# Moving the parameter and state rows ahead of the second weight unit, halving the first unit, and scaling one tile of x on ScalarE, in a hybrid decoder step

## The reference

```python
def mixer(h, conf_buf, ssm_buf, ssm_h, w_in, ...):
    proj = einsum('bld,de->ble', h, w_in)              # 1024 -> 2*1024 + 1024 + 1536 + 16 columns
    u = u_a * sigmoid(u_b)                             # conformer gate
    v, conf_buf_new = causal_dwconv(conf_buf, u, conf_dw_w, conf_dw_b)      # width 31
    v = silu(layernorm(v, conf_ln_g, conf_ln_b))
    xbc_c, ssm_buf_new = causal_dwconv(ssm_buf, xbc, ssm_conv_w, ssm_conv_b) # width 4
    y, h_new = ssd_scan(...)                           # chunked state-space scan
    out = einsum('ble,ed->bld', concat([v, y_ssm]), w_out)
    ...
x = x + mixer(rmsnorm(x, ln_mix))
x = x + hier_moe(rmsnorm(x, ln_ffn))                   # 32 experts of 3 x 1024 x 512, two per token
y = rmsnorm(x, ln_final)
```

## Time and profile before

| what | value |
|---|---|
| median of 3 runs | 794.14 us (793.25 to 794.57) |
| span of the profiled execution, first to last instruction | 789.4 us |
| TensorE busy in it | 757.8 us (96%), granted clock 0.987 in the mean |
| VectorE, ScalarE, GpSimd busy | 270.5, 154.4, 140.3 us |
| DMA | 249.58 MB, 316 GB/s in the mean |

### The profile page before, as it was taken

How to read it: one execution, slowest core, us unless ns; L and a number is a source line. 1 busy time by engine, 2 the same in 40 slices (tenths; PEclk the granted TensorE clock), 3 DMA queues, 4 the chain that set the end, 5 groups by cost and what they waited for, 6 DMA issues and landing times.

```text
span 789.4 us, 8694 instructions
## 1 busy us (share of the span) xinstructions
PE 757.8 (96%) x3470; PEld 360.5 (46%) x3470; DVE 270.5 (34%) x629; ACT 154.4 (20%) x308; POOL 140.3 (18%) x168
## 2 busy tenths in 40 slices
PE   6999999999999999799999999999999999989896
PEld 4667677767843335434333333333333333333332
DVE  2399499985656423511101101110110011011003
ACT  3211121245712003202011112101111110110122
POOL 2279998612002000100000000000000000000000
PEclk9999999999999999799999999999999999999998
DMA  9990610042659786999999999999999999999982
GB/s 312 304 364 10 230 40 1 9 107 108 188 213 275 252 306 237 368 374 414 429 426 427 425 429 425 425 430 426 427 427 426 425 426 427 427 429 425 429 356 69
DMA packets 51400, 249.58 MB, mean 316 GB/s; under 512 B 6982, under 2 KB 24422, under 8 KB 38671
## 3 DMA queue, kind: packets, MB, share of 16 engines
q1 hardware_dynamic: 45460, 243.40, 77.2%
q10 hardware_dynamic: 3371, 2.81, 1.2%
q0 software_dynamic: 2528, 2.79, 1.1%
HBM read 246.87 MB, written 8.61 MB: 324 GB/s over the span
## 4 chain that ended last, share of the span: by engine, by line
PE 91%; DMA 3%; DVE 2%; SPq 2%; issue 2%; ACT 1%; POOLq 0%; DVEq 0%
PE bank L1213 28%; PE bank L810 18%; PE bank L1236 14%; PE bank L1076 9%; PE bank L1261 9%; DMA xcx<-in_state_conf_conv 2%; PE bank L1196 2%; SPq L491 1%; PE bank L1225 1%; PE bank L1065 1%; PE bank L1034 1%; PE bank L905 1%; PE bank L1214 1%; PE bank L1122 1%; PE bank L1047 0%
## 5 line engine op out<-in xcount | busy, mean ns | idle before, releaser
L810 PE MATMUL bank<-region_a,ring 128*128 128x320 f32 x576 | 157.2, 433 | 1.0 <-DMA ring<-in_w_in 1.0
L1654 DVE TENSOR_TENSOR region_a<-region_a,bank 64x512 f32<-64x512 f32 (+1 forms) x33 | 22.5, 680 | 377.6 <-ACT region_a L1581 377.6
L1214 PE MATMUL bank<-ring,zz 128*64 128x512 f32 x320 | 145.4, 610 | 0.0
L1213 PE MATMUL bank<-ring,zz 128*64 128x512 f32 x288 | 127.3, 595 | 2.7 <-issue 2.7
L810 PEld LDWEIGHTS bank<-region_a,ring 128*128 128x128 f32 x576 | 108.7, 190 | 46.3 <-DVE region_a L1654 1.1
L1655 DVE SCALAR_TENSOR_TENSOR bank<-region_a,par,bank 128x256 f32<-128x256 f32 x232 | 91.2, 479 | 0.0
L763 POOL DMA_INDIRECT region_a<-hn_scratch,region_a x16 | 15.9, 996 | 369.6 <-PE bank L1196 355.8
L1261 PE MATMUL bank<-zz,masks 128*128 128x512 f32 (+1 forms) x192 | 77.2, 603 | 0.7 <-ACT zz L1587 0.7
L1213 PEld LDWEIGHTS bank<-ring,zz 128*64 128x64 f32 x288 | 38.1, 137 | 82.5 <-issue 81.7
L1076 PE MATMUL bank<-ring,x_v_y 128*128 128x512 f32 (+1 forms) x192 | 74.0, 605 | 0.0
L1581 ACT ACTIVATE region_a<-bank 64x512 f32<-64x512 f32 x32 | 18.9, 590 | 271.5 <-PE bank L1214 271.5
(11 more groups left out here) (313 smaller groups left out, 770.1 us busy)
## 6 DMA issues: line engine op xcount, KB each, us to landing
ring<-in_expert_w_up SPq DMA_DIRECT2D x20, 2048.0 KB, 24.4
ring<-in_expert_w_gate SPq DMA_DIRECT2D x17, 2048.0 KB, 30.3
ring<-in_expert_w_down SPq DMA_DIRECT2D x16, 2048.0 KB, 34.8
ring<-in_w_in SPq DMA_DIRECT2D x9, 2048.0 KB, 15.7
x_v_y<-in_expert_w_down SPq DMA_DIRECT2D x6, 2048.0 KB, 33.5
x_v_y<-in_expert_w_gate SPq DMA_DIRECT2D x5, 2048.0 KB, 34.6
ring<-in_w_out SPq DMA_DIRECT2D x4, 2048.0 KB, 10.0
xcx<-in_expert_w_gate SPq DMA_DIRECT2D x4, 2048.0 KB, 31.8
```

The lines of the kernel that those rows point to most:

```text
L810: ins = pe.matmul(pt[0:m, 0:T], w[:, k, :], ht[:, k, :], start=k == 0, stop=k == KD - 1)
L1213: pe.matmul(to[0:CAP, :], x[:, k, :], wg[:, FE * k:FE * k + FE], **st)
L1214: ins = pe.matmul(to[CAP:P, :], x[:, k, :], wu[:, FE * k:FE * k + FE], **st)
L1654: tt_ = lambda out, a, b, op: dve.tensor_tensor(out, a, b, op)
```

## The change

Three edits. The first unit of `w_in` is loaded by two transfers of 1 MB, chunks 0 to 3 (semaphore `first_unit`) and chunks 4 to 7 (`ring_in[0]`); tile b0 waits for the first before its chunk 0 and for the second before its chunk 4. The ten parameter and state transfers are issued behind unit 0 in place of unit 1, so ahead of unit `ua0`. The third tile of x (64 tokens) is scaled by ScalarE; VectorE takes its reciprocal between the two halves of `x_gain(0)` and signals it with `rinv_in`.

```diff
@@ load_unit, SyncE
+                if n == 0:
+                    sp_.dma_start(dst[:, 0:KD // 2, :], src[:, 0:KD // 2, :]).then_inc(S("first_unit"), 16)
+                    dst, src = dst[:, KD // 2:, :], src[:, KD // 2:, :]
                 sp_.dma_start(dst, src).then_inc(ring_in[n % R], 16)
...
             for n in range(n_o0 + 1):
                 slot_free(n)
                 load_unit(n)
-                if n == 1:
+                if n == 0:
...
@@ project, TensorE
                 pt = take(pe, *name)
+                first = name == ("in", "b", 0)
                 if unit is None:
                     w, m = wdt, H
+                elif first:
+                    pe.wait_ge(S("first_unit"), 16)
+                    w, m = ring[:, 0, :].rearrange("p (k c) -> p k c", k=KD)[:, :, 0:P], P
                 else:
...
                 for k in range(KD):
+                    if first and k == KD // 2:
+                        landed(pe, unit)
                     ins = pe.matmul(pt[0:m, 0:T], w[:, k, :], ht[:, k, :], start=k == 0, stop=k == KD - 1)
...
@@ ScalarE
+            act.wait_ge(S("rinv_in"), 1)
+            act.activation(xt[0:TS, 2, :], xt[0:TS, 2, :], ACT.Copy, scale=rst[0:TS, 5:6]).then_inc(S("xn"), 1)
 
             act.wait_ge(ring_in[0], 16)
...
@@ VectorE
-            def x_gain(r):
+            def x_gain(r, halves=range(2)):
                 n = TILES[r][1]
-                for q in range(2):
+                for q in halves:
...
             dve.wait_ge(S("mix_in"), 16)
-            x_gain(0)
-            x_scaled(2)
+            x_gain(0, [0])
+            dve.wait_ge(S("rt"), 3)
+            dve.reciprocal(rst[:, 5:6], rst[:, 2:3]).then_inc(S("rinv_in"), 1)
+            x_gain(0, [1])
             x_gain(1)
             x_gain(2)
```

## The result

| kernel | median | runs | ratio to before (95% interval) |
|---|---|---|---|
| before | 793.69 us (790.15 to 794.57) | 4 | |
| changed | 804.63 us (803.04 to 808.73) | 4 | 1.0144 (1.0118 to 1.0171) |

The kernel before was timed once more here, so its median is not quite the 794.14 us of the first three runs. The change costs 10.9 us of the median. The span of its profiled execution is 801.3 us, where before had 789.4, a difference of 11.9.

A forecast was written before the change was run, and what follows sets the result against it. TensorE, busy 757.8 of 789.4 us, was taken as the bound; its wait for `ua0` adds 8.65 us and the clock 1.7, so 794.14 + 10.35 = 804.5 us, range 798.5 to 806.5.

The forecast's parts named there:

- The order of landing decides: SyncE's queue lands transfers in issue order, so with the rows ahead `ua0` lands last and TensorE waits some 11 us.
- the formula: Shift of the next projection after the transposes: landing time of `ua0` minus 23.25, giving +8.65 us.
- L: The time at which unit `ua0` lands in the changed kernel: 31.9 us taken, bounds 21.3 to 31.9.
- The floor of 3.4 us for the rows: Least time for the rows on the slowest engine if spread evenly: 1.3 MB at a unit's 387 GB/s.
- rival C: Rows delay `ua0` only by their bytes; it lands at 21.3 us, run time 792.2 or 791.2; chance 0.10.
- One slow engine: The rows are unevenly spread over the DMA engines; one engine's backlog of 13.5 us sets when they land.
- Clock: TensorE's wait of some 11 us drops its clock to 1.2 GHz, costing 1.7 us, bounds 0 and 2.7.
- The first unit in halves and ScalarE's scaling: First projection starts near 12.0 us, 0.5 us earlier, worth nothing in the end as a0 waits for `ua0`.
- The shift is passed on: None of the early delay is taken up by later slack in the convolutions or experts; it reaches the end whole.
- Span and median: The median stands 4.7 us above the profiled span, so 794.14 + 10.35 gives 804.5 us.

The follow-up runs named there:

- e1: The changed kernel with the ten row transfers issued behind unit `ua0` again, the other two edits kept: 793.52 us, ratio 1.0006.
- e2: The kernel before with only the ten row transfers moved ahead of unit `ua0`: 804.71 us, ratio 1.0149.
- e6: The changed kernel with ScalarE's small transfers (dt bias, a_log, d_skip, ln_ffn, dt columns) issued behind tile a1: 813.09 us, ratio 1.0240.
- e7: The changed kernel with the 31 conv weight rows loaded as 16 + 15 and ScalarE's small transfers issued behind tile a1: 806.63 us, ratio 1.0166.
- e3: The changed kernel with the 31 rows of conv weights loaded as 16 + 15 in two transfers: 801.45 us, ratio 1.0095.
- e5: The kernel before with the 24 state rows loaded as 23 + 1 in two transfers, same place behind `ua0`: 800.52 us, ratio 1.0083.
- e8: The kernel before with only the 31 conv weight rows loaded as 16 + 15, in their old place behind `ua0`: 792.19 us, ratio 0.9993.

## Why the prediction was right, point by point

- **The order of landing decides (right).** The wait moved from the rows to `ua0`, and the shift at the next projection, 12.30 us, is made of the terms that were foreseen: 8.65 from the formula, 1.75 from the clock (10.48 - 8.73), and 1.9 that was missed in L. e1 and e2 show that the order of the rows alone makes the loss.
- **L (mis-sized).** I took 31.9 and gave 31.0 to 32.5 as its range, because the work between `ub0` and `ub1` on the slowest engine is the same in either order. It was 33.8, and `ub1` came at 39.6 in place of 37.6. The stretch from `ub0` to `ua0` took 21.0 us, where before it was 19.5 from `ub0` to the rows, and `ub0`'s second half came 0.3 later. e2, with the rows ahead of `ua0` too, has `ua0` at 33.8 again. So the order may not be quite neutral. That the small transfers, worth 1.4 to 3.0 us behind the rows (e6), cost less beside `ua0`, which they met before, would fit, but it is argued only. And part of it can be spread between executions: the rows landed at 33.06 in e1, in the order of before.
- **The floor of 3.4 us for the rows (wrong).** It was a unit's pace. Loaded together the rows moved at 232 GB/s, so the floor is 5.6 us, and rival C was not to be had even with a nearly even spread: in e7, with the split and without the small transfers, `ua0` landed at 25.7, still behind the 23.25 where gain turns to loss.
- **One slow engine (right, and now shown)** by e3 (7.4 us less for 116 KB taken off) and e5 (6.9 us more for 132 KB put on, and a stretch in which one engine's worth of the queue was at work). The 8.7 us that the prediction had estimated for the 206 KB from the Trainium skill's rule and a unit's pace was too low, as the measured 13.5 had said. The rule of the spread agrees with the runs; the pace is what failed, since an engine also serves the small transfers and, by the figures of e5 and e7, moves its rows more slowly while the others load rows.
- **Clock (right, closer than the method allows).** 1.7 predicted, 1.75 measured. It was read from one wait of 1.9 us and held for one of 13. The other runs show how much of that was luck: the tiles behind the wait lost 1.8 us in e7 (wait 2.6 us), 3.1 in e3 (3.9), 2.6 in e6 (9.1) and 1.9 in e2 (10.5), and in e5 the transposes and the tiles behind them 2.8 (8.7). The bounds given, 0 to 2.7, would not have held e3 and e5.
- **The first unit in halves and ScalarE's scaling (right).** The first matmul began at 11.95, predicted 12.0; the wait for the weights is gone there. Worth nothing in the end, as said: e1 and e2 show it from both sides.
- **The shift is passed on (right for this size).** 12.3 us at 47 us became 11.9 in the spans. For a gain of 2 us the same step did not hold in e8's profile.
- **Span and median (wrong step, small effect).** I put 4.7 us outside the span, from the median of before and the span of one execution. In the profiled execution of the changed kernel it is 803.04 - 801.3 = 1.7 us, and 1.8 in its other runs. The kernel before has 1.7 to 1.9 outside its span in every run made beside the experiments. So its profiled execution was a short one, near 791.1 and 2.6 under the median. The forecast, 10.35 above the median, met the measured 10.9 because the 1.9 missed in L and a difference of 1.0 to 1.4 between spans and medians pull in opposite ways. That the forecast is only 0.1 us off the measured median is luck.

## What to carry to other kernels

Before transfers are reordered on a queue, find out from issue and landing which of them take long for their bytes: a load of 31 rows of 4 KB held one DMA engine for some 5 us (an estimate from 12 rows in 2 us in e5), and the unit issued behind such rows landed after that, however large the mean bandwidth. Whoever moves such a transfer ahead only moves its wait, and to a worse place if what is overtaken is wanted earlier; splitting it (31 rows into 16 + 15) brought the unit behind it 7.4 us earlier and made no kernel slower. And a gain of one or two microseconds at the start is not yet one at the end where later stretches wait too, by amounts that differ between executions, and the clock can fall at such a wait.

## What the runs showed of the hardware

- A transfer that is held by one engine can starve the others. In the changed kernel the DMA share went down to 0.21 and 0.29 from 24 to 28 us while SyncE's issue of the next unit was held. In e5 it went down to 0.11, with one engine at 25 GB/s, although all the rows had been issued.
- Rows of 4 and 6 KB, one to a partition, moved at 232 to 236 GB/s at a full share, where units in pieces of 2 KB move at 387. One engine with 4 KB rows and the others idle made 25 GB/s (e5), a sixteenth of 387 being 24.
- After 13 us without work TensorE ran at the lower clock for its first 3 us or so, 1.75 us lost, no more than after a wait of 1.9 us; after 3.9 us (e3) it did so for its first 6 us, 3.1 us lost. The loss did not grow with the wait.
- The first projection tiles ran at half rate for their first microseconds in five of the ten profiles (e1, e2, e3, e6 and e7), at a cost of 1.8 to 2.2 us, and at full rate in the others. In e2 and e6 the clock reads 0.50 there. In e1, e3 and e7 it reads 1.00 all the same: e1's stretch from 13 to 15 us has three matmul rows to the microsecond, where the kernel before has five or six. The stretches of e1:

```profile
13.00:14.00 1.00, 1.00 (x3) 0.64 (x2) 0.00 (x0) 0.00 (x0) 0.00 (x0) 1.00 1.04 383
14.00:15.00 1.00, 1.00 (x3) 0.67 (x2) 0.00 (x0) 0.00 (x0) 0.00 (x0) 1.00 1.06 391
```
